# Two-layer hybrid decoder trunk on one core: layer 0's step-16 key rows stored from SBUF, and 15 of 16 rows copied in 7680-byte packets

## The reference, cut to what matters

```
kk = jnp.concatenate([k_buf, k], axis=1)
vv = jnp.concatenate([v_buf, v], axis=1)
o = dilated_attention(q, kk, vv, k_buf.shape[1])
n_keep = min(MAX_WINDOW, kk.shape[1])
new_k = kk[:, -n_keep:]
new_v = vv[:, -n_keep:]
```

## Time and profile before

| | before |
|---|---|
| median of 3 runs | 405.16 us |
| the profiled execution | 401.24 us |
| its span | 399.4 us |
| granted TensorE clock, mean | 0.93 |
| TensorE busy | 344.5 us (86%) |
| VectorE busy | 231.7 us (58%) |
| ScalarE busy | 99.4 us (25%) |
| DMA | 158.10 MB, 396 GB/s; HBM read 141.58 MB, written 104.42 MB |

### The profile page before, as it was taken

One profiled execution on the slowest core, in us unless ns is written; L12 is line 12 of the kernel. 1 busy time (PEld: TensorE's weight loads), 2 busy tenths in 40 slices (PEclk: granted clock), 3 DMA queues, 4 the chain that ended last, 5 costly groups with the idle time before them and its releaser, 6 DMA issues.

```text
span 399.4 us, 4715 instructions
## 1 busy us (share of the span) xinstructions
PE 344.5 (86%) x1546; PEld 270.8 (68%) x1546; DVE 231.7 (58%) x524; ACT 99.4 (25%) x234; POOL 53.5 (13%) x102
## 2 busy tenths in 40 slices
PE   2799699999798869899949999997979877989990
PEld 1588488887576646688738888885647654658880
DVE  1604679889858974610132589847994997441110
ACT  3300114433523314210020021541352222230011
POOL 8400500060003300033000410006000030000000
PEclk9789989999879889999969999998978988989997
DMA  7999999999999999999999999999999999999993
GB/s 288 416 416 402 420 416 415 419 418 410 417 421 418 394 413 397 391 417 400 399 419 419 418 395 415 418 418 419 418 422 416 406 365 344 372 390 390 384 387 130
DMA packets 45157, 158.10 MB, mean 396 GB/s; under 512 B 6820, under 2 KB 20062, under 8 KB 45134
## 3 DMA queue, kind: packets, MB, share of 16 engines
q0 software_dynamic: 14976, 87.28, 54.1%
q10 hardware_dynamic: 14394, 41.52, 26.2%
q1 hardware_dynamic: 15764, 29.02, 19.5%
HBM read 141.58 MB, written 104.42 MB: 616 GB/s over the span
## 4 chain that ended last, share of the span: by engine, by line
SPq 33%; PE 23%; DMA 21%; DVE 9%; ACTq 5%; issue 3%; ACT 3%; DVEq 0%
SPq L469 23%; DMA kg<-in_cache_k_win 10%; DMA out<-kg 10%; PE pj L668 9%; SPq L449 8%; PE pj L811 8%; ACTq L848 3%; DVE yc L1250 2%; SPq L523 2%; DMA cst<-in_const 2%; PE ptr L593 1%; DVE ssc L1194 1%; DVE tok L1188 1%; PE psc L740 1%; PE psc L593 1%
## 5 line engine op out<-in xcount | busy, mean ns | idle before, releaser
L668 PE MATMUL pj<-hT,wt 128*128 128x264 f32 x800 | 198.4, 407 | 5.4 <-DVE hT L1108 5.3
L668 PEld LDWEIGHTS pj<-hT,wt 128*128 128x128 f32 x800 | 159.3, 202 | 38.5 <-issue 10.1
L1250 DVE SCALAR_TENSOR_TENSOR yc<-u_ext,par,yc 128x256 f32<-128x256 f32 x180 | 77.3, 481 | 3.5 <-DVE mix L1143 0.8
L811 PE MATMUL pj<-mix,wt 128*128 128x264 f32 x256 | 61.1, 395 | 0.0
L811 PEld LDWEIGHTS pj<-mix,wt 128*128 128x128 f32 x256 | 49.2, 195 | 8.4
L582 POOL DMA_DIRECT2D out<-in_cache_v_win x48 | 26.2, 555 | 155.3 <-issue 155.3
L582 POOL DMA_DIRECT2D out<-in_cache_k_win x48 | 26.0, 550 | 115.8 <-issue 115.8
L1320 DVE TENSOR_TENSOR xT<-xT,pj 128x264 f32<-128x264 f32 x16 | 6.9, 429 | 55.2 <-PE pj L811 55.2
L925 ACT ACTIVATE ex<-pj 128x264 f32<-128x264 f32 x22 | 8.6, 391 | 77.7 <-issue 44.2
L1188 DVE TENSOR_TENSOR tok<-kg,qb 128x1536 f32<-128x1536 f32 x10 | 17.6, 1758 | 6.3 <-DMA kg<-in_cache_k_win 5.9
L1134 DVE SCALAR_TENSOR_TENSOR u_ext<-ex,pj 128x256 f32<-128x256 f32 x6 | 2.5, 422 | 29.1 <-ACT ex L925 29.1
(11 more groups left out here) (175 smaller groups left out, 324.3 us busy)
## 6 DMA issues: line engine op xcount, KB each, us to landing
wt<-in_w_tiles ACTq DMA_DIRECT2D x62, 512.0 KB, 31.3
out<-in_cache_k_win POOLq DMA_DIRECT2D x24, 1080.0 KB, 70.0
out<-in_cache_v_win POOLq DMA_DIRECT2D x24, 1080.0 KB, 79.5
out<-in_cache_k_win POOLq DMA_DIRECT2D x8, 1200.0 KB, 80.3
out<-in_cache_v_win POOLq DMA_DIRECT2D x8, 1200.0 KB, 77.3
out<-in_cache_k_win POOLq DMA_DIRECT2D x16, 432.0 KB, 73.5
out<-in_cache_v_win POOLq DMA_DIRECT2D x16, 432.0 KB, 79.2
kg<-in_cache_k_win SPq DMA_DIRECT2D x32, 144.0 KB, 32.3
```

The lines of the kernel that those rows point to most:

```text
L668: last = nc.tensor.matmul(pj[n % RING][:, 0:T], wt[:, g % WRING, k, :], hT[:, k, :], start=(k == 0), stop=(k == KD - 1))
L811: last = nc.tensor.matmul(pj[n % RING][:, 0:T], wt[:, g % WRING, k, :], mix[:, k, :], start=(k == 0), stop=(k == KD - 1))
L1250: last = V.scalar_tensor_tensor(out=yc[:, t, 0:SEQ], in0=x_w, scalar=par[:, ROW_CW + w * CT + t:ROW_CW + w * CT + t + 1], in1=yc[:, t, 0:S ...
```

## The change

The pair of keys and layer 0 enters `DEEP`. With it, for layer 0's keys:

- GpSimd's two pieces of 720 and 800 rows of a sample become two of 768 rows of which 15 of 16 are copied, in packets of 7680 B (`DEEP_BYTES` gets an entry for each pair; those of layer 1 stay as they were). The DMA for the last 15 rows (L588) goes; the one for layer 0's values stays.
- `store_rows` issues, for each of the 8 samples, two more DMAs on SyncE's queue: L453 (120 KB) and L455 (22.5 KB).
- Before it gathers layer 1's keys, SyncE waits for the landing of these 16 stores too (`k_deep_out`, L537 and L538).

```
--- before.py
+++ after.py
@@ -205,7 +205,7 @@
-DEEP = (("k", 1), ("v", 1))
+DEEP = (("k", 0), ("k", 1), ("v", 1))
@@ -221,7 +221,7 @@
-DEEP_BYTES = {"k": (DEEP_STEP - 1) * C_ATT * 4 // 4, "v": (DEEP_STEP - 1) * C_ATT * 4 // 3}
+DEEP_BYTES = {step: (DEEP_STEP - 1) * C_ATT * 4 // (4 if step == ("k", 1) else 3) for step in DEEP}
@@ -575,7 +575,7 @@
                     elif (kind, l) in DEEP:
-                        size = DEEP_BYTES[kind]
+                        size = DEEP_BYTES[(kind, l)]
```

## The result

The changed kernel took 419.56 us as the median of 4 runs (419.42 to 424.07), the kernel before 404.96 in its 4 (402.5 to 406.25): a ratio of 1.039, 95% interval 1.0351 to 1.0428. It is slower, by 16 us as the ratio has it and by 14.6 between the two medians. The profiled execution took 419.42 us, its span is 417.6 us, 18.2 more than before's.

The account below looks back on a forecast made before the run. The prediction took SyncE's ordered queue, pacing layer 1, as the bound. Its terms, +26 queue, -2 given back, -4 tail, +0.2 DMA time, made +20 us: 421 profiled, 424 median, range 409 to 440 (8 in 10).

Parts of the forecast that it names:

- The bound: SyncE's one ordered queue paces layer 1; parameters, keys and values arrive late or just in time, without slack.
- Price of a place in the queue: SyncE's queue ahead of layer 1: 1008 added packets at 37.5 per us, taken as 26 us, bounds 18 to 32.
- The wait for landed stores: SyncE before layer 1's key gather: waiting for the added stores too adds nothing of its own.
- What is late next: Layer 1: parameters 26 us late at 228 us, keys 24 us late at 296, values about 24 late at 359.
- The two delays aren't added: Layer 1's parameters and keys: the keys' delay of 24 us contains the parameters' 26 us, so they don't sum.
- The tail: After the last y store: GpSimd's copies are done early, y stores meet empty queues; 4 us off, bounds 0 and 6.
- GpSimd's half: GpSimd's queue: 128 packets and one 180 KB DMA fewer, on no chain, worth nothing except at the tail.
- DMA time: DMA engines: 2.9 us of 16 engines leave GpSimd's copies, 3.1 come with SyncE's stores; net +0.2 us, neutral.
- the rule of HBM's bytes: Whole kernel: time would follow HBM bytes, 1.17 of 246 MB fewer giving 1.9 us off, 403 us; the prediction argued against it.
- 1 (DMA time decides): Rival for the whole kernel: DMA time, not places in a queue, decides; +0.2 us, 405 us; chance 0.09.
- 2 (faster): Rival at the kernel's end: GpSimd's stream sets it, fewer packets end it 6 us earlier, 399 us; chance 0.05.
- 3 (delays add up): Rival in layer 1: parameter stop of 26 us, further key wait and lower clock, about 15 more, 445 us; chance 0.09.

Follow-up runs that it names:

- states_late: Kernel before, with layer 0's two state copies moved from ahead of its key stores in SyncE's queue to layer 1's place: 404.74 us, ratio 0.9987.
- stores_only: Kernel before, with the same 16 DMAs added on SyncE's queue, into a scratch tensor, and the wait for them: 424.90 us, ratio 1.0538.
- short_rows: Changed kernel, storing only the first 512 B of each of the 760 rows, same packet count: 420.59 us, ratio 1.0441.
- few_packets: Changed kernel, same bytes with 5 slots of a partition as one 7680 B piece, into a scratch tensor, 512 packets fewer: 411.85 us, ratio 1.0221.
- pieces_5760: Changed kernel, with GpSimd copying layer 0's keys in packets of 5760 B instead of 7680 B: 409.57 us, ratio 1.0196 to the kernel before.
- copies_only: Changed kernel without SyncE's layer 0 deep key stores and the wait for them, 95 rows per sample unwritten: 399.62 us, ratio 0.991.

## Why the prediction was right

**The bound.** Right for the side that the change loads: three waits on SyncE's transfers without slack, and all three moved by 24 to 25 us. It left out that the DMA engines were a floor beside it. "Neither is alone the bound" named the 9 tenths, but the sum used them in the tail only. On the slower side nothing else hangs on it; a forecast for a change that takes packets away from SyncE would have failed on it, as the top of what I expected of states_late (6 us) did.

**Price of a place in the queue.** 26 us for 1008 packets; measured 24.7 at the parameters, and 28.0 in stores_only. The issue of the last store came 28.1 us late, and 3.4 of them were given back while SyncE issued the parameters and they landed, ahead of TensorE's stop, where the prediction had put nothing; it had put its 2 us of giving back behind the stop, where 0.6 came (24.7 to 24.1). That the sum still fits is in part luck. q1 grew by 1008 packets exactly; 248 of them are the completion words that were reckoned. That the count of SyncE's own packets decides and not their bytes is shown by short_rows and few_packets from both sides. The bytes of the neighbours' packets do count, since they stand in every turn: that is pieces_5760.

**The wait for landed stores** adds nothing of its own: the gather started 27.0 us later (189.99 to 216.95), the last store's issue 28.1 us later (151.74 to 179.82).

**What is late next.** Parameters 228 forecast, 227.0 measured; keys 296, 295.9, with a wait of 7.99 us where 4 was forecast; values 359, 360.2. "The two delays aren't added" holds, by the three runs in which nobody waits for the keys, though my own test of it missed: the parameters' issue lies in the shadow of the stores' landing, which the prediction hadn't seen.

**The tail.** -4 forecast, -5.2 measured, by the mechanism named: the y stores meet empty queues. It doesn't belong to either half, since copies_only has a tail of 2.8 us and stores_only one of 3.1: it shortens wherever the last y store comes after the floor. **GpSimd's half**: put at nothing but the tail; copies_only gives 0.9% by itself. Its "some 250 fewer" packets were 192: the 128 are right, and the DMA for the last rows was 64 packets and not some 100.

**DMA time.** The term "+0.2 us, neutral" is wrong as a measurement: packet time of the three queues was 99.8% of 399.4 = 398.6 us of 16 engines, and is 97.6% of 417.6 = 407.6. q0 moved 1.17 MB less in the same time. As the engines are idle at the end this decided nothing. By the rule of HBM's bytes the time would have been 403 us; 1.17 MB fewer were read, and the kernel became slower, with 586 GB/s instead of 616.

**Rivals.** 1 (DMA time decides) fell with stores_only and short_rows. 2 (faster) has its place in copies_only and was outweighed. 3 (delays add up) fell: keys 24, not 40 us later, and the mean granted clock went from 0.93 to 0.925 between the profiled executions (0.906 to 0.91 in the changed kernel's other three).

**The number.** 421 for a profiled execution, 419.42 measured. 424 for the median, 419.56 measured: the profiled execution of before lay 3.7 us below its median and the changed one's at it. Adding the sum to the median of before rather than to the profiled time was the larger part of the miss of 4 us. Seen the other way, +20 was forecast, and it was +18.2 between the profiled executions and +14.6 between the medians.

## What to carry to other kernels

Where several queues are full at once, price a transfer by the packets that it puts ahead of somebody's wait, completion words included, not by its bytes: here 1 us for some 40 (36 to 43, by the size of the neighbours' packets). Before moving an instruction in a queue, look for the wait whose shadow it fills. And check how far the second bound lies: a gain on one chain ends at the other's floor, a loss doesn't.

## What was not expected of the hardware

- The share of busy time and the bytes moved don't go together. In the changed kernel's 385 to 399 us (columns as in the earlier trace rows) nearly all packets are of small stores (ScalarE's queue 1229, SyncE's 505, GpSimd's 72):

```profile
385.00:399.00 14.00, 14.00 (x69) 11.87 (x69) 1.30 (x4) 0.00 (x0) 0.00 (x0) 1.00 0.75 232
```

A share of 0.75 moved 232 GB/s; at 1.02 it had been 418 in the earlier trace rows, 410 per unit of share against 309 here. In the records of before's trace a packet's time goes by its size: the median is 291 ns for 7680 B, 159 for 4096 B, 65 for 1536 B and 9 for a completion word. In a turn of 426 ns the word saves 56 ns against a row of 1536 B, and it costs its queue the same turn.

- A neighbour's packet size helps to set a queue's speed: 43 packets per us beside packets of 5760 B, 36 beside those of 7680 B, with ScalarE's queue not always full in the first.
- A full queue holds its issuing engine: two stores took ScalarE 7.49 us instead of 1.24 us, and its compute waited behind them.
